# Small TensorE steps of one stage moved in among the tiles of another

## The reference

```
h = rmsnorm(x);  proj = h @ w_in
# latent attention: 16 heads, scores over 128 + 64 channels, softmax, values
p = softmax(mask(q @ k.T * scale));  o = p @ v
x = x + (sigmoid(..) * o + sigmoid(..) * sgu) @ w_out
# expert layer
h2 = rmsnorm(x)
q = h2 @ w_pq                       # 2048 -> 8 heads x 2 x 128
sub = q @ peer_keys                 # [tokens, 8, 2, 128]
s, i = top_k(sub, 16)               # for each head and half
cand = s[0][:, None] + s[1][None];  top_s, pos = top_k(cand, 16)
idx = i[0][pos // 16] * 128 + i[1][pos % 16];  gate = softmax(top_s)
a = gelu(h2 @ peer_u[idx]) * gate;  x = x + a @ peer_v[idx]
```

## Time and profile before

| | busy, us | share |
|---|---|---|
| TensorE matmul | 3658.2 | 97% |
| VectorE | 2683.6 | 71% |
| ScalarE | 1779.1 | 47% |
| GpSimd | 144.9 | 4% |

### The profile page before, as it was taken

How to read it: one execution, slowest core, us unless ns; L and a number is a source line. 1 busy time by engine, 2 the same in 40 slices (tenths; PEclk the granted TensorE clock), 3 DMA queues, 4 the chain that set the end, 5 groups by cost and what they waited for, 6 DMA issues and landing times.

```text
span 3774.0 us, 49824 instructions
## 1 busy us (share of the span) xinstructions
PE 3658.2 (97%) x17330; PEld 3058.0 (81%) x17330; DVE 2683.6 (71%) x3515; ACT 1779.1 (47%) x2118; POOL 144.9 (4%) x210
## 2 busy tenths in 40 slices
PE   8999999999899999999999997999999899999998
PEld 7888888888788888888888886877788688888886
DVE  5654567669797777777778885788876556666566
ACT  5554444444454434443434444546654345545453
POOL 4000000000000000000000000010000000000000
PEclk9999999999999999999999998999999899999999
DMA  7546558756568988888878874554446456655653
GB/s 243 161 147 199 191 180 283 268 179 213 171 229 342 338 299 312 296 312 300 319 269 280 278 251 153 171 168 155 153 157 201 134 179 187 189 186 185 192 185 123
DMA packets 210255, 828.01 MB, mean 219 GB/s; under 512 B 23792, under 2 KB 24304, under 8 KB 196528
## 3 DMA queue, kind: packets, MB, share of 16 engines
q1 hardware_dynamic: 177488, 640.23, 51.3%
q10 hardware_dynamic: 14400, 102.77, 7.2%
q0 software_dynamic: 18208, 82.84, 5.9%
HBM read 787.48 MB, written 38.27 MB: 219 GB/s over the span
## 4 chain that ended last, share of the span: by engine, by line
PE 90%; DVE 4%; ACT 3%; issue 2%; DMA 0%; POOL 0%; ACTq 0%; DVEq 0%; POOLq 0%
PE ps L2176 27%; PE ps L2178 27%; PE ps L2177 27%; PE ps L2464 2%; ACT hi L680 1%; DVE lo L1231 1%; PE ps L2242 1%; PE ps L2244 1%; PE ps L2243 1%; PE ps L2597 1%; PE ps L2490 1%; PE ps L2585 1%; PE ps L2257 1%; PE ps L2201 1%; PE ps L2701 0%
## 5 line engine op out<-in xcount | busy, mean ns | idle before, releaser
L1231 DVE TENSOR_TENSOR lo<-raw,hi 128x1024 fp32r<-128x1024 f32 (+1 forms) x1217 | 1480.3, 1220 | 986.9 <-ACT hi L680 984.0
L680 ACT CAST hi<-raw 128x1024 fp32r<-128x1024 f32 (+1 forms) x1217 | 1273.9, 1048 | 1827.2 <-PE ps L2178 1781.4
L2176 PE MATMUL ps<-hi,xh 128*128 128x512 f32 x2880 | 1143.5, 397 | 10.4 <-DVE lo L1231 6.3
L2178 PE MATMUL ps<-hi,xl 128*128 128x512 f32 x2880 | 1126.7, 391 | 0.0
L2177 PE MATMUL ps<-lo,xh 128*128 128x512 f32 x2880 | 1126.1, 391 | 0.0
L2176 PEld LDWEIGHTS ps<-hi,xh 128*128 128x128 f32 x2880 | 544.5, 189 | 123.6 <-issue 4.6
L2178 PEld LDWEIGHTS ps<-hi,xl 128*128 128x128 f32 x2880 | 543.7, 189 | 115.1
L2177 PEld LDWEIGHTS ps<-lo,xh 128*128 128x128 f32 x2880 | 544.4, 189 | 110.6
L2176 PE MATMUL ps<-hi,Ph 128*128 128x512 f32 x1024 | 401.8, 392 | 0.0
L2178 PE MATMUL ps<-hi,Pl 128*128 128x512 f32 x1024 | 399.0, 390 | 0.0
L2177 PE MATMUL ps<-lo,Ph 128*128 128x512 f32 x1024 | 398.6, 389 | 0.0
(11 more groups left out here) (435 smaller groups left out, 3647.6 us busy)
## 6 DMA issues: line engine op xcount, KB each, us to landing
raw<-in_peer_u SPq DMA_DIRECT2D x256, 512.0 KB, 4.7
raw<-in_peer_v SPq DMA_DIRECT2D x256, 512.0 KB, 4.4
mraw<-in_w_mod ACTq DMA_DIRECT2D x96, 1024.0 KB, 6.2
raw<-in_w_up SPq DMA_DIRECT2D x176, 512.0 KB, 3.5
raw<-in_w_in SPq DMA_DIRECT2D x144, 512.0 KB, 3.6
raw<-in_in SPq DMA_DIRECT2D x128, 512.0 KB, 3.5
raw<-in_w_down SPq DMA_DIRECT2D x88, 512.0 KB, 4.2
raw<-in_out SPq DMA_DIRECT2D x64, 512.0 KB, 4.2
```

The costliest lines, as they stand in the source:

```text
L680: SC.copy(hi[:, n0 % SPL, 0:w], raw[:, n0 % RAW, 0:w]).then_inc(hi_ready, 1)
L1231: V.tensor_tensor(lo[:, n0 % SPL, 0:w], raw[:, n0 % RAW, 0:w], hi[:, n0 % SPL, 0:w].bitcast(F32), ALU.subtract).then_inc(lo_ready, 1)
L2176: PE_.matmul(acc, xhi[:, k0 + k, xs], H, start=s0, stop=False)
L2178: mm = PE_.matmul(acc, xlo[:, k0 + k, xs], H, start=False, stop=s1)
```

## The change

- `query_turn` and `sub_scores`: the eight transposes of `Q` and the eight score groups no longer stand behind the projection. Two of each stand behind tiles 2, 3 and 5, 6 of chunks 1 to 3 (for the chunk before), and the last two behind tiles 1, 2 and 4, 5 of expert block 0. The scores use banks 6 and 7 only. `sub` and `sub2` change places.
- The modulation sums stand behind tile 6 of block 0. VectorE does five splits, then waits for them and for the scores, and starts the selection; the rounds carry 3+1, 3+1, 2+1 and 2 splits instead of 2+1 each.
- `ahead_bank`: block 0 uses banks 0, 1, block 1 banks 4, 5, the others as before.
- The gates' exponential stands at tile 5 of block 9 on ScalarE; the normalisation on VectorE ahead of the splits of block 10's last tiles; selection's turn behind tile 2 of block 10, its copies at tile 3.
- Latent heads: `probsT` at 3k+4, `values` at 3k+6, `soft_out` at 3k+7 (at most 15).

```diff
--- before.py
+++ after.py
@@ -101,6 +101,10 @@
+def ahead_bank(b):
+    return {0: 0, 1: 4}.get(b, 2 * ((b + 1) % 2))
 def bias_slot(i):
@@ -214,8 +218,8 @@
         keys = at("keys", [P, 16, NKEY], W0 + 32)
-        sub = at("sub", [P, 32, NKEY], W0 + 40)
-        sub2 = at("sub2", [P, 32, NKEY], W0 + 56)
+        sub = at("sub", [P, 32, NKEY], W0 + 56)
+        sub2 = at("sub2", [P, 32, NKEY], W0 + 40)
         vals = at("vals", [P, 32, TOPK], W0 + 72)
@@ -773,7 +777,7 @@
                         probs(GROUP * r + k)
-                    if i == 3 * k + 3:
+                    if i == 3 * k + 4:
                         probsT(GROUP * r + k)
@@ -875,12 +879,26 @@
+            def query_turn(g):
+                act.wait_ge(qt_ps, g + 1)
+                SC.copy(QT[:, 2 * g:2 * g + 2], ps[:, 4 + g % 2].rearrange("p (k t) -> p k t", k=2)
+                        ).then_inc(qt_ok, 1)
+            def sub_scores(g):
+                act.wait_ge(sub_ps, g + 1)
+                SC.copy(sub[:, 4 * g:4 * g + 4].rearrange("p a n -> p (a n)"), ps[:, 6 + g % 2]
+                        ).then_inc(sub_ok, 1)
             for pair in range(2):
...
                             mod2_load(8 + 2 * (2 * pair + ab) + j // 4)
+                        if pair + ab and j in (2, 3):
+                            query_turn(2 * (2 * pair + ab) + j - 4)
+                        elif pair + ab and j in (5, 6):
+                            sub_scores(2 * (2 * pair + ab) + j - 7)
                         if pair + ab == 0 and j in (1, 2):
@@ -891,14 +909,6 @@
-            for g in range(8):
-                act.wait_ge(qt_ps, g + 1)
-                SC.copy(QT[:, 2 * g:2 * g + 2], ps[:, 4 + g % 2].rearrange("p (k t) -> p k t", k=2)
-                        ).then_inc(qt_ok, 1)
-            for g in range(8):
-                act.wait_ge(sub_ps, g + 1)
-                SC.copy(sub[:, 4 * g:4 * g + 4].rearrange("p a n -> p (a n)"), ps[:, 4 + g % 4]
-                        ).then_inc(sub_ok, 1)
             n0 = BASE["peer"]
@@ -910,15 +920,21 @@
             for b in range(CHOICE):
-                splits(n0 + b * TC, TC)
-                gelu(b, n0 + b * TC + TC, 2 * ((b + 1) % 2))
-            act.wait_ge(gate_in, 1)
-            SC.activation(sel[:, 2], sel[:, 2], ACT.Exp).then_inc(gate_exp, 1)
-            act.wait_ge(selT_ps, 1)
-            act.wait_ge(sel_ok, 1)
-            for i in range(3):
-                SC.copy(selT[:, i], ps[:, 4 + i, 0:S]).then_inc(selT_ok, 1)
+                for j in range(TC):
+                    split(n0 + b * TC + SPL + j)
+                    if b == 0 and j in (1, 2):
+                        query_turn(5 + j)
+                    elif b == 0 and j in (4, 5):
+                        sub_scores(2 + j)
+                    elif b == CHOICE - 2 and j == 5:
+                        act.wait_ge(gate_in, 1)
+                        SC.activation(sel[:, 2], sel[:, 2], ACT.Exp).then_inc(gate_exp, 1)
+                    elif b == CHOICE - 1 and j == 3:
+                        act.wait_ge(selT_ps, 1)
+                        act.wait_ge(sel_ok, 1)
+                        for i in range(3):
+                            SC.copy(selT[:, i], ps[:, 4 + i, 0:S]).then_inc(selT_ok, 1)
+                gelu(b, n0 + b * TC + TC, ahead_bank(b))
@@ -1364,7 +1380,7 @@
                         soft_in(GROUP * r + k)
-                    if i == 3 * k + 6:
+                    if i == min(3 * k + 7, 15):
                         soft_out(GROUP * r + k)
@@ -1546,17 +1562,17 @@
                     mod2_unit(8 + 2 * (j // TC) + j % TC // 4)
+            early = [BASE["peer"] + SPL]
+            def stream():
+                split(early[0])
+                early[0] += 1
+            for _ in range(5):
+                stream()
             dve.wait_ge(mod_ps, 1)
             V.tensor_tensor(mcol[:, 5], ps[:, 7, 0:KD], C("bmod", 5 * KD, KD), ALU.add).then_inc(mod_col, 1)
-            early = [BASE["peer"] + SPL]
-            def stream():
-                split(early[0])
-                early[0] += 1
             dve.wait_ge(sub_ok, 8)
@@ -1628,17 +1644,20 @@
                                             f5[:, t, :, q].unsqueeze(2).to_broadcast([P, PH, TOPK, TOPK]), ALU.mult))
-                    stream()
-                    stream()
+                    for _ in range((3, 3, 2, 2)[2 * q + t]):
+                        stream()
                     st.link(V.tensor_reduce(sel[:, q, t].rearrange("p (h k) -> p h k", h=PH), eq[:], AX, ALU.add))
-                    stream()
-            while early[0] < BASE["peer"] + 2 + CHOICE * TC:
+                    if 2 * q + t < 3:
+                        stream()
+            while early[0] < BASE["peer"] + SPL + (CHOICE - 1) * TC:
                 stream()
...
                             ).then_inc(sel_ok, 1)
+            while early[0] < BASE["peer"] + 2 + CHOICE * TC:
+                stream()
@@ -2283,9 +2302,9 @@
                         scores(GROUP * r + k)
-                    if i == 3 * k + 3:
+                    if i == 3 * k + 4:
                         probsT(GROUP * r + k)
-                    if i == 3 * k + 5:
+                    if i == 3 * k + 6:
                         values(GROUP * r + k)
@@ -2405,12 +2424,9 @@
-            chunk(BASE["pq"], 0, TC, 0, PB["pq"], xh, xl, before=h2_ready, after=h2_last)
-            for c in range(1, 4):
-                chunk(BASE["pq"] + c * TC, 0, TC, c % 2, PB["pq"] + c // 2, xh, xl)
-            pe.wait_ge(acc_free[0], 2 * (PB["pq"] + 2))
-            pe.wait_ge(acc_free[1], 2 * (PB["pq"] + 2))
-            for g in range(8):
+            def query_turn(g):
+                c = g // 2
+                pe.wait_ge(acc_free[c % 2], 2 * (PB["pq"] + c // 2) + 2)
                 if g >= 2:
@@ -2419,40 +2435,69 @@
                 mm.then_inc(qt_ps, 1)
-            pe.wait_ge(mod2_used, KD)
-            for k in range(KD):
-                mm = PE_.matmul(ps[:, 7, k:k + 1], macc2[:, k * P:(k + 1) * P], ones[:, 0:1], start=True, stop=True)
-            mm.then_inc(mod_ps, 1)
-            pe.wait_ge(keys_in, 16)
-            pe.wait_ge(qt_ok, 8)
-            for g in range(8):
-                if g >= 4:
-                    pe.wait_ge(sub_ok, g - 3)
-                if g == 3:
-                    pe.wait_ge(mod_col, 1)
+            def sub_scores(g):
+                pe.wait_ge(keys_in, 16)
+                pe.wait_ge(qt_ok, g + 1)
+                if g >= 2:
+                    pe.wait_ge(sub_ok, g - 1)
                 for j in range(4):
                     hp, t = 2 * g + j // 2, j % 2
-                    mm = PE_.matmul(ps[:, 4 + g % 4, j * P:(j + 1) * P], QT[:, hp, t * P:(t + 1) * P], keys[:, hp],
+                    mm = PE_.matmul(ps[:, 6 + g % 2, j * P:(j + 1) * P], QT[:, hp, t * P:(t + 1) * P], keys[:, hp],
                                     start=True, stop=True)
...
+            def query_steps(c):
+                def step(j):
+                    if j in (2, 3):
+                        query_turn(2 * c + j - 4)
+                    elif j in (5, 6):
+                        sub_scores(2 * c + j - 7)
+                return step
+            chunk(BASE["pq"], 0, TC, 0, PB["pq"], xh, xl, before=h2_ready, after=h2_last)
+            for c in range(1, 4):
+                chunk(BASE["pq"] + c * TC, 0, TC, c % 2, PB["pq"] + c // 2, xh, xl, after=query_steps(c))
+            pe.wait_ge(acc_free[0], 2 * (PB["pq"] + 2))
             n0 = BASE["peer"]
-            def u_block(n, off=0, bank=0):
+            def u_block(n, off=0, bank=0, after=None):
                 for j in range(TC):
                     tile(n + j, off, xh, xl, SL * j, bank, j == 0, j == TC - 1)
+                    if after is not None:
+                        after(j)
+            def last_queries(j):
+                if j in (1, 2):
+                    query_turn(5 + j)
+                elif j in (4, 5):
+                    sub_scores(2 + j)
+                elif j == 6:
+                    pe.wait_ge(mod2_used, KD)
+                    pe.wait_ge(sub_ok, 8)
+                    for k in range(KD):
+                        mm = PE_.matmul(ps[:, 7, k:k + 1], macc2[:, k * P:(k + 1) * P], ones[:, 0:1],
+                                        start=True, stop=True)
+                    mm.then_inc(mod_ps, 1)
+            def choice_turn(j):
+                if j == 2:
+                    pe.wait_ge(sel_ok, 1)
+                    for i in range(3):
+                        for t in range(TT):
+                            mm = PE_.transpose(ps[:, 4 + i, t * P:(t + 1) * P], sel[:, i, t], ident)
+                    mm.then_inc(selT_ps, 1)
             for b in range(CHOICE):
-                if b >= 2:
+                if b == 1:
+                    pe.wait_ge(qt_ok, 8)
+                elif b:
                     pe.wait_ge(a_ok, b * 2 - 2)
-                u_block(n0 + b * TC, 0, 2 * ((b + 1) % 2))
-            pe.wait_ge(sel_ok, 1)
```

(12 more changed lines are left out.)

## The result

The changed kernel takes 3746.14 us (median of 4 runs, 3745.18 to 3747.52) against 3774.54 us (4 runs): a ratio of 0.9925 [0.9907, 0.9942]. It saves 28.4 us where 16.3 were forecast, and lies 2.9 us under the range's lower end. The profiled execution took 3747.52 us, 28.1 less than the one of before.

A forecast was written before the change was run, and what follows sets the result against it. TensorE, busy 97% of 3774.0 us, was taken as the bound, leaving idle and lower-clock stretches to save. Savings of 12.8 (projection to one-hots) and 3.5 (heads) made 16.3 us: 3759.3 profiled, 3758.3 median, range 3749 to 3766.

The forecast's parts named there:

- the falls behind the sums: Expert stage and block 0: lower clock follows one-column modulation sums; 3.4 us at each place, 3.4 charged for the moved sums.
- the fall put on top of the waits: End of the selection: the two nearby idles of 2.2 and 1.8 us bring a clock fall of 1.7 us, bounds 0 and 3.4.
- place A: End of the query projection, 743.15 to 763.20: transposes, modulation sums and score matmuls; clock fall there before, 1.7 us.
- A and B: From the query projection's end to the one-hots behind block 10: 278.3 us becomes 265.5, 12.8 saved.
- C: Latent heads, TensorE's 7.9 us of waits for `pr`: 3.5 us saved, bounds 1 and 9.6; new `qrr` waits of 1.8.
- Stalls of the selection: TensorE idle 2.2 us at tile 82 and 1.8 ahead of selection's turn; 4.0 together, bounds 0 and 9.
- The work itself, 256 us out of rows: Projection's end to first one-hots: turns, score groups, sums, selection's turn, 88 tiles and first one-hot pair total 256.4 us.
- the two waits counted whole: Latent heads: the two `pr` waits with no rotation behind them go whole, 1.8 us together.
- The selection was not the bound: Rival at the end of block 10: VectorE enters the rounds late, `sel` wait takes 8 to 10 us more; 3767, chance 0.08.
- the heads' waits did not go whole: Rival in the latent heads: their waits vanish whole, giving 8.5 to 9.6 us; 3753, chance 0.16.
- the small fp32 groups: Rival in chunks 1 to 3 and block 0: they lower the clock, 3.4 us per pair, 27 us; 3785, chance 0.03.
- The one whose time came nearest, 3743: Rival, everything hidden: heads' waits whole, no stall at tiles 82 and 83, no clock fall; 3743, chance 0.04.

The follow-up runs named there:

- e9: The changed kernel run again unaltered, beside other kernels on one chip; 3747.81 us, ratio 0.9933.
- e12: The kernel before with only the expert stage's four runs of modulation sums put four behind each of four tiles, their copy earlier; 3762.07 us, ratio 0.9973.
- e1: The kernel before with only the latent heads' steps one tile on; 3763.84 us, ratio 0.998.
- e2: The changed kernel with the latent heads' steps put back as before; 3755.95 us, ratio 0.996.
- e3: The kernel before with only the queries' turns, scores and modulation sums among tiles, and block 0's banks; 3765.62 us, ratio 0.9986.
- e4: The changed kernel with the modulation sums of block 0 and the expert stage put four behind each of four tiles; 3743.72 us, ratio 0.9924.
- e6: The changed kernel with one split more in the selection's third round and its turn behind tile 4 of block 10; 3746.84 us, ratio 0.9939.
- e7: The changed kernel with the modulation sums spread over tiles and VectorE's copy `mcol` one step earlier; 3743.92 us, ratio 0.9927.
- e10: The changed kernel with soft_out(0) behind the gates' sum, soft_in ahead of soft_out at one position, and four statistics slots; 3748.5 us, ratio 0.9934.
- e11: The changed kernel with soft_out(0) behind the gates' sum, selection rounds 4, 4, 4, 2, turn behind tile 4, and sums spread; 3732.66 us, ratio 0.9893.

## Why the prediction was wrong

**The step that failed is the clock**, in two forms: the falls behind the sums, and (under the stalls, below) the fall put on top of the waits. The forecast took the falls behind one-column sums as a price of the code: "there are four such places in the expert stage and all lose as much", so it kept 13.7 us of them in the time after and charged 3.4 for the sums it moved. They are drawn anew in each execution, 0, 1.7 or 3.4 us each. The profiled run of before had drawn the most of all profiles, and that of after 8.5: 5.2 us of the missing 11.8 (28.1 - 16.3), in code that nobody edited. e9 shows that the same code costs other amounts in other executions, e12 that these falls come and go with the sums in one piece. The moved sums cost 1.7 instead of 3.4, which is a draw too: they cost 1.7 in five profiles and 3.4 in two. For place A the forecast read the fall behind the sums as theirs; e1 has it ahead of them, behind the wait for `Q`. Part of the 28.4 is such a draw as well: the three other groups have medians of 3771.0 to 3773.0 for the kernel before, and e9 saves 25.1 against its own. Even that is 8.8 over the forecast.

By place, the missing 11.8 are 4.9 in unedited code behind the first one-hots, 3.3 in A and B, 2.3 in C and 1.2 ahead of every edit, within 0.1. By cause, about 9 of it is clock (5.2 there, 3.4 in A and B, 0.6 in C).

**Stalls of the selection**: forecast 2.2 at tile 82 and 1.8 ahead of the turn, measured 1.93 and 1.48. This working, from the rounds on VectorE, held to 0.6 us. The 1.7 us of clock put on top was wrong even where the fall came, as in e9: it stands in front of the second wait and lies inside it. The two prices should not have been added.

**A and B**: 16.1 instead of 12.8. The clock gives 1.7 (the moved sums) + 1.7 (no fall at the stalls) and the stalls 0.6, 4.0 together; the remainder, 0.7 the other way, is in the work (0.3 of it a wait for the one-hots). A score group took 0.81 us up to the next tile's start, with that tile's first matmul 0.09 longer: 0.90 for the 0.94 charged. The work itself, 256 us out of rows, was the sound part.

**C**: 5.8 instead of 3.5. The mechanism is as forecast. TensorE's timeline in the heads after, with `probsT` that no longer waits and the turn of `qrr` that does:

```profile
150.95 0.49 PE L2285 MATMUL ps<-const,pr 128*128 128x128 f32 x3
...
163.80 0.66 PE L2366 MATMUL ps<-const,qrr 128*128 128x128 f32 x4 [1.27 <-DVE qrr L1347]
...
216.97 0.66 PE L2366 MATMUL ps<-const,qrr 128*128 128x128 f32 x4 [1.29 <-DVE qrr L1347]
...
270.14 0.66 PE L2366 MATMUL ps<-const,qrr 128*128 128x128 f32 x4 [1.28 <-DVE qrr L1347]
```

The new wait is there three times, at 1.3 where 1.8 was forecast. What was mis-sized is what a round saves: the way from one `qrr` turn to the next went from 53.78 us (221.16 - 167.38) to 53.17, 0.6 for the forecast 0.2; in the first of the three it is 54.83 to 52.42, 2.4 us, of which 0.8 is one of the two waits counted whole. The rest of C is the clock: the fall of the fourth round went whole (1.7 for 1.1), and no new wait of 1.3 us brought one in any profile. That the part is worth 8.5 in the medians (e1) may in part go back to falls in the heads: the four profiles of kernels with the heads as before (before, e2, e3, e12) lose 1.7, 3.4, 3.4 and 1.7 us there; after, e1, e4, e6, e7, e9, e10 and e11 lose none.

**The start**, 1.2 us ahead of every edit, is a difference between two executions (e9's is 0.6).

**The rivals**: none of them came. The selection was not the bound, the heads' waits did not go whole, and the small fp32 groups brought no fall with 4 or 8 records together (the changed kernel's first fall begins at 769.9, behind the sums of block 0). The one whose time came nearest, 3743, gets there by other terms. The range failed since it was put together from what the change does, with the unchanged falls at no width at all; with the 9.3 us that four draws cost on average (4 x 2.3) in place of 13.7 it would have reached some 5 us further down, an estimate from the nine profiles. What stays open is what decides a draw.

## What to carry to other kernels

A profile is one draw: before a lower clock in a stretch is charged or kept, compare the same code in other rounds and other executions, and give unchanged code a width of its own. Sixteen one-column matmuls in a row are worth spreading among full tiles; it gave 10.9 us here in an otherwise unchanged kernel, and its runs lay 4.0 us apart instead of 6.3. Where a gain of 2 to 3 us is at stake amid draws of 8, read it from two fixed points of the trace, with the falls between them counted, and not from medians; the single gains then added up (7.7 read, 7.4 found).

## What the hardware showed that was not expected

- The granted clock falls behind 16 one-column matmuls with TensorE busy for 13.00 of 13 us, by 0, 1.7 or 3.4 us, and not behind four groups of 4 with full tiles between (24 places in five profiles; in e12 the clock is 1.00 from 1030 to 2270 us).
- At the lower level a matmul of 512 columns starts 0.43 us behind the last, and at the higher 0.23; 3 us of it ahead of a wait of 1.48 us changed no start behind the wait (e9).
- The idle stretches of 1.3 us ahead of the `qrr` turns were followed by no fall in any of the six profiles that have three each (after, e1, e4, e6, e7, e9); the twelve waits of 2.04 us there, in the four profiles of kernels that keep the heads as before, were followed by six falls of 1.7 us.
